# The decay matrices of a state-space layer: the mask held at zero on ScalarE, selections over 128 partitions, one bank handed on later

## The reference, cut to what matters

```
seg = acs[..., :, None] - acs[..., None, :]
causal = jnp.tril(jnp.ones((l, l), dtype=bool))
decay = jnp.exp(jnp.where(causal, seg, -jnp.inf))
cb = jnp.einsum('bclgn,bcsgn->bcgls', cc, bc)
y_diag = jnp.einsum('bcgls,bcgkls,bcsgkp->bclgkp', cb, decay, x)
...
y_off = jnp.einsum('bclgn,bcgkpn,bcgkl->bclgkp', cc, prev, jnp.exp(acs))
```

## Time and profile before

| what | value |
| --- | --- |
| median of 3 runs | 1293.94 us (1293.35 to 1294.14) |
| profiled execution, its own time | 1293.49 us |
| span of its instructions | 1291.7 us |
| mean granted TensorE clock | 0.993 |
| PE, DVE, ACT, POOL busy | 97%, 49%, 54%, 76% of the span |
| the four groups' side work | about 716 to 880 us of the span |

### The profile page before, as it was taken

How to read it: one execution, slowest core, us unless ns; L and a number is a source line. 1 busy time by engine, 2 the same in 40 slices (tenths; PEclk the granted TensorE clock), 3 DMA queues, 4 the chain that set the end, 5 groups by cost and what they waited for, 6 DMA issues and landing times.

```text
span 1291.7 us, 22605 instructions
## 1 busy us (share of the span) xinstructions
PE 1256.3 (97%) x9023; PEld 1152.5 (89%) x9023; DVE 628.9 (49%) x1477; ACT 701.8 (54%) x1308; POOL 983.6 (76%) x774
## 2 busy tenths in 40 slices
PE   6999999999999999998999999999999999999997
PEld 6988899988899888888999988989999988888886
DVE  5666755557656444412655577742024334444312
ACT  5454556455556666544544565664447545666532
POOL 4665668766669999897798766678888757899894
PEclk9999999999999999999999999999999999999998
DMA  6443445444446666665466444446566535665562
GB/s 239 133 129 117 132 136 173 152 142 147 120 134 199 186 184 191 188 182 185 134 194 195 143 129 140 131 132 172 182 182 215 163 115 159 186 192 183 178 195 82
DMA packets 57784, 208.92 MB, mean 162 GB/s; under 512 B 6352, under 2 KB 7632, under 8 KB 57424
## 3 DMA queue, kind: packets, MB, share of 16 engines
q1 hardware_dynamic: 57680, 207.48, 53.0%
HBM read 206.41 MB, written 1.05 MB: 161 GB/s over the span
## 4 chain that ended last, share of the span: by engine, by line
PE 90%; DVE 6%; ACT 2%; issue 1%; DMA 1%; SPq 0%; DVEq 0%
PE bank L382 21%; PE bank L355 16%; PE bank L357 16%; PE bank L356 16%; PE bank L385 11%; PE bank L880 1%; PE bank L669 1%; DVE ar L941 1%; DMA raw<-w_dram 1%; PE bank L2095 1%; PE bank L2067 1%; PE bank L2117 1%; PE bank L2069 1%; PE bank L2068 1%; PE bank L1715 1%
## 5 line engine op out<-in xcount | busy, mean ns | idle before, releaser
L315 POOL TENSOR_TENSOR wlo<-raw,whi 128x512 fp32r<-128x512 f32 x770 | 983.4, 1305 | 292.5 <-ACT whi L307 290.7
L307 ACT ACTIVATE whi<-raw 128x1024 fp32r<-128x1024 f32 x387 | 404.3, 1053 | 32.9 <-PE bank L357 12.4
L355 PE MATMUL bank<-xx,whi 128*128 128x256 f32 (+1 forms) x1320 | 387.8, 294 | 11.8 <-DVE xx L418 9.5
L357 PE MATMUL bank<-xx,wlo 128*128 128x256 f32 (+1 forms) x1320 | 376.3, 285 | 0.0
L356 PE MATMUL bank<-xx,whi 128*128 128x256 f32 (+1 forms) x1320 | 376.2, 285 | 0.0
L355 PEld LDWEIGHTS bank<-xx,whi 128*128 128x128 f32 x1320 | 252.0, 191 | 21.2 <-issue 14.2
L356 PEld LDWEIGHTS bank<-xx,whi 128*128 128x128 f32 x1320 | 251.9, 191 | 0.5
L357 PEld LDWEIGHTS bank<-xx,wlo 128*128 128x128 f32 x1320 | 252.2, 191 | 0.0
L382 PE MATMUL bank<-xx,whi 128*128 128x512 f32 x704 | 178.9, 396 | 0.0
L355 PE MATMUL bank<-yy,whi 128*128 128x256 f32 (+1 forms) x524 | 151.3, 289 | 0.0
L357 PE MATMUL bank<-yy,wlo 128*128 128x256 f32 (+1 forms) x524 | 149.0, 284 | 0.0
(11 more groups left out here) (263 smaller groups left out, 1403.5 us busy)
## 6 DMA issues: line engine op xcount, KB each, us to landing
raw<-w_dram SPq DMA_DIRECT2D x387, 512.0 KB, 3.6
h<-x_dram SPq DMA_DIRECT2D x2, 544.0 KB, 6.3
cst<-con_dram SPq DMA_DIRECT2D x1, 1049.0 KB, 10.4
ar<-mem_dram SPq DMA_DIRECT2D x1, 1024.0 KB, 5.9
out_dram<-h SPq DMA_DIRECT2D x4, 256.0 KB, 2.5
cst<-con_dram SPq DMA_DIRECT2D x1, 134.0 KB, 3.7
prm<-par_dram SPq DMA_DIRECT2D x1, 131.0 KB, 3.5
```

Source lines behind the costliest of these rows:

```text
L307: e.activation(whi[:, i % NSPL, :], raw[:, i % NRAW, :], ACT.Copy).then_inc(*whi_done.done(i))
L315: return e.tensor_tensor(wlo[:, q, c0:c1], raw[:, i % NRAW, c0:c1], whi[:, q, c0:c1].bitcast(F), ALU.subtract)
L355: e.matmul(o, wh, both[:, 0, :], start=(i == 0), stop=False)
L357: m = e.matmul(o, wl, both[:, 0, :], start=False, stop=(i == len(feed) - 1))
```

## The change

The mask matmuls go, with the bf16 identity and mask that DVE built once in the first layer. `acr` and `idr`, the operands of the selection, grow from 64 to 128 partitions; the upper 64 are set to zero by one ACT instruction at the mixer's start. ACT now does four instructions `relu(acs_s - acs_t)` (scale -1, bias the token's own sum), which hold the fall at zero where the mask stood, then one exp of minus that over 512 columns, after a wait for its own last instruction. Both follow E8 in the same step, where exp stood one step later. The product with C·B on DVE, whose C·B already carries the causal zeros, is unchanged. DVE's negation `negA` goes. The `gr` bank of groups 0 to 2 is given back in the next group's step after `st`, not ahead of its transposes; a `seg` bank is named as given right after it is taken.

```diff
-            e.tensor_copy(identb, ident)
-            e.tensor_scalar(maskb, cst[:, C_CM:C_CM + 256], 1.0, -NEG, ALU.subtract, ALU.mult).then_inc(
-                *v_step.done("mask"))
...
-        e.tensor_scalar(negA, tokm[:, 2:4, :], -1.0, None, ALU.mult).then_inc(*v_step.done("negA"))
...
     def steps_scalar(e):
+        e.activation(tens["acr"][64:128, :], cst[64:128, C_COS:C_COS + S + 32], ACT.Copy, scale=0.0).then_inc(
+            *s_high.done("zero"))
...
     def ssd_tensor(e, g):
-        for hp in range(5):
-            if hp:
-                e.wait_ge(*s_step.of("E", g, hp - 1))
-                for i in range(2):
-                    m = e.matmul(o[:, S * i:S * i + S], identb, maskb, start=False, stop=True, skip_group_check=True)
-                m.then_inc(*piece.done("mask", g, hp - 1))
-                side_.give(("seg", g, hp - 1), (s_step, ("M", g, hp - 1)))
-            if hp < 4:
-                o = side_.take(e, "seg", g, hp)
...
-                    m = e.matmul(o[:, S * i:S * i + S], idr[:, hd:hd + 1].broadcast_to([64, 128]), acr, start=(i == 0),
-                                 stop=False, skip_group_check=True)
+        if held:
+            held.pop()()
+        for hp in range(4):
+            o = side_.take(e, "seg", g, hp)
+            side_.give(("seg", g, hp), (s_step, ("M", g, hp)))
+            e.wait_ge(*v_low.of("acr"))
+            for i in range(2):
+                hd = 8 * g + 2 * hp + i
+                m = e.matmul(o[:, S * i:S * i + S], idr[:, hd:hd + 1].broadcast_to([128, 128]), acr, start=True, stop=True)
+            m.then_inc(*piece.done("seg", g, hp))
+            yield
...
-        side_.give(("gr", g), (v_step, ("yn", 4 * g + 3)))
+        give = lambda: side_.give(("gr", g), (v_step, ("yn", 4 * g + 3)))
+        held.append(give) if g < 3 else give()
...
     def ssd_scalar(e, g):
-                e.wait_ge(*piece.of("mask", g, hp - 1))
-                e.wait_ge(*v_step.of("negA"))
-                        m = e.activation(M[:, 2 * (hp - 1) + i, 128 * c:128 * c + 128],
-                                         o[:, S * i + 128 * c:S * i + 128 * c + 128], ACT.Exp, bias=negA[:, c, hd:hd + 1])
...
+            e.wait_ge(*piece.of("seg", g, hp))
+            e.activation(E8[:, 2 * hp:2 * hp + 2, :], o.rearrange("p (a s) -> p a s", a=2)[:, :, 128:256],
+                         ACT.Exp).then_inc(*s_step.done("E", g, hp))
...
+                    m = e.activation(M[:, 2 * hp + i, 128 * c:128 * c + 128], o[:, S * i + 128 * c:S * i + 128 * c + 128],
+                                     ACT.Relu, scale=-1.0, bias=tokm[:, 2 + c, hd:hd + 1])
+            m.then_inc(*s_step.done("fall", g, hp))
+            e.wait_ge(*s_step.of("fall", g, hp))
+            e.activation(M[:, 2 * hp:2 * hp + 2, :], M[:, 2 * hp:2 * hp + 2, :], ACT.Exp, scale=-1.0).then_inc(
+                *s_step.done("M", g, hp))
+            yield
```

More of the change, by code:

```diff
@@ L251, in build @@
     spare = cst[:, C_R3 + 9:C_R3 + 10]
-    identb, maskb = tens["cnb"][:, 0:128], tens["cnb"][:, 128:384]
     rows = [tens["rows"][:, i, :] for i in range(2)]
@@ L1474, in ffn_scalar @@
         residuals_scalar(e, K.nxt)
-    (zacc, xs0, xs1, bc0, bc1, zs0, zs1, xdt, btok, xw, prev, M, E8, cv0, cv1, cv2, mt0, mt1, mt2, tokm, negA, acol) = arena(
+    (zacc, xs0, xs1, bc0, bc1, zs0, zs1, xdt, btok, xw, prev, M, E8, cv0, cv1, cv2, mt0, mt1, mt2, tokm, acol) = arena(
         (8, S), (4, S), (4, S), (2, S), (2, S), (4, S), (4, S), (2, 512), (128,), (512,), (512,), (8, 256),
-        (8, 128), (S,), (S,), (S,), (S,), (S,), (S,), (5, 32), (2, 32), (1,))
+        (8, 128), (S,), (S,), (S,), (S,), (S,), (S,), (5, 32), (1,))
     xsT, BC, zs = [xs0, xs1], [bc0, bc1], [zs0, zs1]
@@ L1676, in silu_vector @@
                 *v_step.done("cvx", cb))
+    held = []
     def ssd_tensor(e, g):
@@ L1702, in ssd_tensor @@
         e.matmul(o, btok, xw, start=True, stop=True).then_inc(*piece.done("st", g))
-        for hp in range(5):
-            if hp:
-                e.wait_ge(*s_step.of("E", g, hp - 1))
-                for i in range(2):
-                    m = e.matmul(o[:, S * i:S * i + S], identb, maskb, start=False, stop=True, skip_group_check=True)
-                m.then_inc(*piece.done("mask", g, hp - 1))
-                side_.give(("seg", g, hp - 1), (s_step, ("M", g, hp - 1)))
-            if hp < 4:
-                o = side_.take(e, "seg", g, hp)
-                e.wait_ge(*v_low.of("acr"))
-                for i in range(2):
-                    hd = 8 * g + 2 * hp + i
-                    m = e.matmul(o[:, S * i:S * i + S], idr[:, hd:hd + 1].broadcast_to([64, 128]), acr, start=(i == 0),
-                                 stop=False, skip_group_check=True)
-                m.then_inc(*piece.done("seg", g, hp))
-                yield
+        if held:
[9 more added lines that the diff above has]
+            yield
         side_.give(("cb", g), (v_step, ("MC", g, 3)))
@@ L1844, in ssd_scalar @@
         e.activation(prev, side_.at("st", g), ACT.Copy).then_inc(*s_out.done("prev", g))
-        for hp in range(5):
-            if hp:
-                o = side_.at("seg", g, hp - 1)
-                e.wait_ge(*piece.of("mask", g, hp - 1))
-                e.wait_ge(*v_step.of("negA"))
-                for i in range(2):
-                    for c in range(2):
-                        hd = 8 * g + 2 * (hp - 1) + i
-                        m = e.activation(M[:, 2 * (hp - 1) + i, 128 * c:128 * c + 128],
-                                         o[:, S * i + 128 * c:S * i + 128 * c + 128], ACT.Exp, bias=negA[:, c, hd:hd + 1])
[L1855 to L1861, removed]
+        for hp in range(4):
+            o = side_.at("seg", g, hp)
+            e.wait_ge(*piece.of("seg", g, hp))
+            e.activation(E8[:, 2 * hp:2 * hp + 2, :], o.rearrange("p (a s) -> p a s", a=2)[:, :, 128:256],
+                         ACT.Exp).then_inc(*s_step.done("E", g, hp))
+            for i in range(2):
+                for c in range(2):
+                    hd = 8 * g + 2 * hp + i
+                    m = e.activation(M[:, 2 * hp + i, 128 * c:128 * c + 128], o[:, S * i + 128 * c:S * i + 128 * c + 128],
[5 more added lines that the diff above has]
+            yield
         yield
@@ L2357, in program @@
             "cst": sb("cst", [128, NCONST]), "prm": sb("prm", [128, NPARAM]), "ar": sb("ar", [128, ARENA]),
-            "cnb": sb("cnb", [128, 384], mybir.dt.bfloat16),
-            "acr": sb("acr", [64, S + 32], R), "sq": sb("sq", [128, 2, T]), "rows": sb("rows", [128, 2, T]),
+            "acr": sb("acr", [128, S + 32], R), "sq": sb("sq", [128, 2, T]), "rows": sb("rows", [128, 2, T]),
             "banks": [ctx.enter_context(nc.psum_tensor(f"bank{i}", [128, 512], F)) for i in range(8)],
```

## The result

The changed kernel takes 1296.15 us (median of 20 runs, 1293.66 to 1297.45) against 1293.8 for the kernel before in the same comparison. The ratio is 1.0017, 95% interval 1.0011 to 1.0023: 0.17% slower, 2.2 us, where 5.4 us faster was forecast; the range ended at 1292.4.

What follows compares the result with a forecast made beforehand. PE was taken to bound the whole, with DVE capping groups 1 and 2. Gains of 0.8 + 2 x 0.4 + 3.8 = 5.4 us took 1293.49 to 1288.1, as median 1288.5; range 1283.5 to 1292.4.

Steps and rivals of the forecast that it cites:

- The state product, the mask pairs and the selection: PE per group: masks gone and selections at the dense rate save 2.5 us; no wait for yn saves 1.33.
- group 3: Beside the sa blocks no bank waits for DVE, so all PE savings are kept: 3.8 us, bounds 2.3 and 4.0.
- Rival (a): PE's selection keeps its price, so less is saved: 3.9 us gain, 1290.0; chance 0.14.
- ACT: Four relu cost as four exp, 1.15 us; new exp 0.6; the extra work is covered beside convolution blocks.
- Rival (d): ACT becomes the bound, tanh of c1 and c3 falls behind DVE's taps: 4.6 us slower, 1298.5; chance 0.06.
- Group 0: ACT leads, its tanh setting cvx of c1 and c3: 0.8 us gained, bounds 0 and 2.5.
- Groups 1 and 2: DVE caps the gain ahead of z1: 0.4 us each; each could lose or win 1.6 us.
- Rival (c): In groups 1 and 2 two more DVE steps held, 1.6 us each group later: gain 2.2, 1291.7; chance 0.14.

Runs made afterwards that it cites:

- e6_only_128: The kernel before with only the selections over 128 partitions, mask matmuls kept; 1299.96 us, ratio 1.0044 to before.
- e7_sel64: The changed kernel with the selection back at 64 partitions and without the zeroing instruction; 1296.16 us, ratio 1.0024 to before.
- e5_only_bank: The kernel before with only the bank of gr handed back later; 1287.91 us, ratio 0.9958 to before.
- e2_fill: The changed kernel with the fourth selection of groups 1 and 2 repeated nine times, same result; 1294.46 us, ratio 1.0007 to before.
- e1_bank_early: The changed kernel with the bank of gr handed back at once, as before; 1291.26 us, ratio 0.9985 to before.
- e12_mc: The changed kernel with DVE's MC and EC one block later and nothing else; 1289.93 us, ratio 0.9972 to before.
- e10_silu_copy: The changed kernel with tanh and cvx ahead of the step's side work and three-column copies read from PSUM; 1283.73 us, ratio 0.9927 to before.
- e3_silu_first: The changed kernel with tanh and cvx of a finished pair ahead of the same step's side work; 1286.49 us, ratio 0.9948 to before.
- e4_copy_psum: The changed kernel with the three-column copies ahead of the taps reading the block's PSUM bank; 1284.38 us, ratio 0.9932 to before.

## Why the prediction was wrong

**The state product, the mask pairs and the selection: right.** 2.5 and 1.33 us per group were forecast; group 3, which keeps all, is 3.9 us shorter (3.8 forecast). The step is 0.48 us where 0.47 was said. Rival (a) is out: the selection over 128 partitions runs at the dense rate in the changed kernel and in e6_only_128. Between e7_sel64 and the changed kernel lie 1.5 us in group 3 for four selections, 0.37 each. So of the two rules of the Trainium skill that the prediction weighed, the drain at a change of tiling mode ("TensorEngine Tiling (Array Packing)", Key Properties) agrees with these rows. The other, by which the row count does not matter for the weight load ("TensorE: Matmul & The Clock Gate", on what happens when a matmul is issued), is not contradicted: the weight loads of the 64-partition selections took 0.18 us, those of 128 partitions 0.19. The prediction had drawn from it that a selection keeps its price, which it does not say; the 0.37 us lie outside the weight load.

**ACT: right.** Relu for exp 1.15 us the four, the new exp 0.63, tanh late for nobody in groups 1 and 2. Rival (d) had the sign, but not the place: ACT is idle while PE waits.

**Group 0: the size right, in part by luck.** -1.2 against -0.8, inside its bounds, and ACT led at c1 as said (DVE waits 2.17 us for its tanh). But at c3 the forecast had ACT's tanh last. It was DVE: its copies were held there (1.33 us for 0.23), it worked without a pause from 729.80 on, and it started cvx at 736.83 without waiting for ACT. The two came out 0.3 us apart once the 0.7 us at the mixer's start are taken off.

**Groups 1 and 2: this step failed.** "So DVE's waits for M, 0.27 at 772.01 and 1.21 at 779.38, go" held, and that PE would wait at z1 for cvx, 3.8 us ahead, held to 0.1. What failed is "Afterwards it is freed 0.27 us earlier, and z1 starts at about 777.6", with its bound "each such group can lose 1.6 or win 1.6 us". Relative to its group's start z1 came 2.1 us later, and each group lost 3.4 to 4.1 us. Two terms make it up. First, held steps: 6.90 us in place of 4.39, less the 0.27 wait and another 0.1, so 2.1 us on the chain (22.57 against 20.45). I had seen the cause, had taken one pair of low parts as its size, and so had stopped at 1.6; low parts, EC and copies were all held. Rival (c) was this mechanism, sized at about half. Second, the clock, which no part of the prediction named: from z1 to z3 PE took 10.6 us in group 1 and 11.3 in group 2, where 9.2 stood before, so 1.4 and 2.1 us. 2.1 + 1.4 = 3.5 and 2.1 + 2.1 = 4.2, where 3.4 and 4.1 us were measured.

The deeper fault is that I treated DVE's chain as a length to be corrected by the waits that go. It is not one: with DVE's program unchanged between them, it was 20.45 (before), 19.13 (e5_only_bank) and 22.60 us (e6_only_128). My forecast moved PE and ACT and kept POOL's halves where they stood. The sum over the rest, -1.2 and -3.9, is 5.1 us; groups 1 and 2 took 7.5 back.

**Left open.** What decides whether the lower clock follows a pause. Ahead of z1 in groups 1 and 2 all eight pauses of about 3.4 us and more in the profiles were followed by it, and five of the nine of 2.0 to 2.7 us: those of 2.1 in e2_fill and not in e1_bank_early, those of 2.0 in e12_mc, not the one of 2.7 in e10_silu_copy, and one of two nearly equal ones in e3_silu_first. That the drop is PE's answer to its own idle time fits the groups with no pause there or one of 1.0 to 1.5 us, where it is not seen, but the runs do not give the rule, and each profile is one execution. That POOL holds DVE (and not another reader of SBUF) is read from the ends of the two engines' instructions, from the steps beside ACT alone and from the copies; no kernel without POOL's work was tried. Why POOL's halves moved as they did is not shown either.

## What to carry to other kernels

Where a second engine, for a stretch, has no idle time ahead of a bank that PE waits for, work taken off PE is worth what that engine's chain to the next bank allows, and a longer wait can cost more than its length when the clock falls behind it. Before such a change, list the second engine's instructions that stretch (the same form at 0.4 and 1.5 us is the sign), sum the whole stretch, and take that sum, both ways, as the bound. Cheap cures come first: give the instruction that frees the bank its place ahead of other work, and give small SBUF copies a PSUM operand.

## What the runs showed of the hardware

- DVE instructions with SBUF operands alone stretched beside POOL from 0.4 to 1.5 us (low parts), 0.41 to 1.5 (EC), 0.15 to 1.27 (a copy of three columns) and 0.68 to 1.77 (product by the decay, 512 columns), and ended a fixed 0.02 to 0.55 us, by their kind, behind the end of one of POOL's halves; those with a PSUM operand (MC, taps, cvx) stayed within 0.03 us in all kernels. POOL's halves stretched in turn, from 1.26 to 1.5 us beside low parts, to 1.75 beside the product by the decay and to 1.95 where the low parts got in first (e4_copy_psum).
- Two 64-partition matmuls amid 128-partition ones cost 0.37 us more than two of 128 partitions (e7_sel64), with weight loads of 0.18 and 0.19 us.
- After 13 of the 17 pauses of PE of 2.0 to 3.9 us ahead of z1 its steps were 0.21 in place of 0.12 us for 2.3 to 5 us, beginning at the restart or up to 1.5 us behind it. Between two groups alike in all else (e3_silu_first) one such stretch cost 1.5 us.
- A pair of groups with the same program repeats to 0.03 us in held time within one execution (6.90 and 6.90, 3.22 and 3.22), except in e10_silu_copy (4.06 and 2.93).
